# mLSTM probabilities times scores: the scores read from PSUM by VectorE instead of from a copy made by ScalarE

## What is computed

```
dmat = where(causal, b[t] - b[s] + i[s], -inf)
s    = einsum('bhtd,bhsd->bhts', q, k) * exp(dmat - mt[t])     # scores times probabilities
num  = einsum('bhts,bhsd->bhtd', s, v) + sc * einsum('bhtk,bhkv->bhtv', q, C)
den  = sum(s) + sc * einsum('bhtk,bhk->bht', q, n)
h    = num / max(|den|, exp(-mt))
```

## Time and profile before

| quantity | us |
|---|---|
| median of 3 runs | 1116.43 |
| lowest and highest of them | 1115.91 and 1117.73 |
| span of the profiled execution, first to last instruction | 1115.5 |
| busy TensorE / VectorE / ScalarE / GpSimd in it | 1048.6 / 317.7 / 196.8 / 97.2 |

### The profile page before, as it was taken

One profiled execution on the slowest core, in us unless ns is written; L12 is line 12 of the kernel. 1 busy time (PEld: TensorE's weight loads), 2 busy tenths in 40 slices (PEclk: granted clock), 3 DMA queues, 4 the chain that ended last, 5 costly groups with the idle time before them and its releaser, 6 DMA issues.

```text
span 1115.5 us, 13239 instructions
## 1 busy us (share of the span) xinstructions
PE 1048.6 (94%) x5164; PEld 440.2 (39%) x5164; DVE 317.7 (28%) x639; ACT 196.8 (18%) x412; POOL 97.2 (9%) x179
## 2 busy tenths in 40 slices
PE   8999999999999999899899999999899988998996
PEld 5667755433433343333233323342324332433332
DVE  6778454421222212121121212121212120202123
ACT  5433613610201020002010201010002000100002
POOL 7887300000000000000000000000000000000000
PEclk9999999999999999999999999999999999999999
DMA  7531689999999999999999999999999999999995
GB/s 235 173 114 33 197 328 379 384 423 429 433 430 428 432 430 432 432 431 432 432 430 431 432 431 432 431 431 432 432 429 432 431 431 432 431 431 432 424 427 211
DMA packets 62051, 429.45 MB, mean 385 GB/s; under 512 B 12022, under 2 KB 25054, under 8 KB 33342
## 3 DMA queue, kind: packets, MB, share of 16 engines
q1 hardware_dynamic: 60868, 428.16, 91.9%
q10 hardware_dynamic: 1146, 0.79, 0.3%
HBM read 424.68 MB, written 3.67 MB: 384 GB/s over the span
## 4 chain that ended last, share of the span: by engine, by line
PE 61%; DMA 35%; DVE 2%; ACT 1%; issue 1%; SPq 1%; ACTq 0%; DVEq 0%
DMA ring_a<-in_exp_w_dram 26%; PE psum L2374 16%; PE psum L2409 13%; DMA ring_b<-in_exp_w_dram 8%; PE psum L2395 7%; PE psum L1825 4%; PE psum L2308 4%; PE psum L2137 3%; PE psum L2331 3%; PE psum L1837 3%; PE psum L2418 1%; PE psum L2258 1%; PE psum L2264 1%; SPq L438 0%; PE psum L2424 0%
## 5 line engine op out<-in xcount | busy, mean ns | idle before, releaser
L2374 PE MATMUL psum<-ring_a,xg 128*64 128x512 f32 x1200 | 341.8, 600 | 14.8 <-DMA ring_a<-in_exp_w_dram 14.8
L2409 PE MATMUL psum<-ring_a,aT 128*64 128x512 f32 x768 | 217.7, 596 | 9.0 <-DMA ring_a<-in_exp_w_dram 8.8
L2374 PEld LDWEIGHTS psum<-ring_a,xg 128*64 128x64 f32 x1200 | 102.9, 137 | 170.4 <-issue 166.5
L2374 PE MATMUL psum<-ring_b,xg 128*64 128x512 f32 x368 | 152.3, 598 | 7.7 <-DMA ring_a<-in_exp_w_dram 7.7
L1640 DVE TENSOR_TENSOR x<-x,psum 128x512 f32<-128x512 f32 x64 | 44.0, 688 | 383.1 <-PE psum L2331 383.1
L2395 PE MATMUL psum<-ring_a,xg 128*64 128x512 f32 x336 | 105.3, 614 | 13.2 <-DMA ring_b<-in_exp_w_dram 13.2
L2409 PEld LDWEIGHTS psum<-ring_a,aT 128*64 128x64 f32 x768 | 68.3, 137 | 110.9 <-issue 105.6
L2409 PE MATMUL psum<-ring_b,aT 128*64 128x512 f32 x256 | 104.1, 595 | 3.6 <-ACT aT L1027 1.8
L1709 DVE TENSOR_SCALAR acts<-psum 128x512 f32<-128x512 f32 x32 | 22.0, 687 | 223.0 <-PE psum L2395 207.7
L2374 PEld LDWEIGHTS psum<-ring_b,xg 128*64 128x64 f32 x368 | 43.1, 136 | 75.4 <-issue 62.7
L1023 ACT ACTIVATE acts<-acts 128x512 f32<-128x512 f32 x32 | 20.1, 627 | 296.1 <-DVE acts L1709 296.1
(11 more groups left out here) (493 smaller groups left out, 943.1 us busy)
## 6 DMA issues: line engine op xcount, KB each, us to landing
ring_a<-in_exp_w_dram SPq DMA_DIRECT2D x144, 2048.0 KB, 26.3
ring_b<-in_exp_w_dram SPq DMA_DIRECT2D x46, 2048.0 KB, 24.8
ring_a<-in_w_in_dram SPq DMA_DIRECT2D x4, 2048.0 KB, 8.6
ring_a<-in_w_out_dram SPq DMA_DIRECT2D x2, 2048.0 KB, 9.5
ring_a<-in_w_in_dram SPq DMA_DIRECT2D x3, 1024.0 KB, 6.0
ring_a<-in_state_ml_c_dram SPq DMA_DIRECT2D x4, 512.0 KB, 6.4
out_dram<-ring_a SPq DMA_DIRECT2D x4, 512.0 KB, 6.5
ring_b<-in_exp_w_dram SPq DMA_DIRECT2D x2, 1024.0 KB, 28.7
```

What stands on the lines that cost most here:

```text
L2374: m = M(psum[64 * x:64 * x + 64, bk, :], xg[:, k, u, 64 * x:64 * x + 64], w[x][:, 512 * bk:512 * bk + 512], start=False, stop=(k == KD - 1))
L2409: m = M(psum[64 * x:64 * x + 64, 4 + nn, :], aT[:, 2 * j + s, 64 * x:64 * x + 64], w[x][:, 1024 * s + 512 * nn:1024 * s + 512 * nn + 512], ...
```

## The change

ScalarE's four copies of `st{h}` into `stS` go, and the buffer `stS` with them, so that two small buffers (`smpS`, `scS`) move to a lower address. VectorE's product reads the scores from the bank itself, waits for the exponential (`mb{h}` drained) and for the fill of `st{h}`, and is now what drains `st{h}`.

```diff
-        stS, smpS, scS = carve(ra, [128, H, 384]), carve(ra, [128, TS]), carve(ra, [128, H, TS])
+        smpS, scS = carve(ra, [128, TS]), carve(ra, [128, H, TS])
...
                 A(E[:, h, 256:384], bank(f"mb{h}")[:, 256:384], ACT.Exp, scale=-1.0, bias=rtok[:, 1, h:h + 1]).then_inc(
                     drained[FILLS[f"mb{h}"][0]], 1)
-                copy_out(f"st{h}", stS[:, h, :], bank(f"st{h}")[:, 0:384])
...
             def e_prob(h):
-                b, f = FILLS[f"st{h}"]
+                b, f = FILLS[f"mb{h}"]
                 dve.wait_ge(drained[b], f + 1)
-                says(TT(E[:, h, :], stS[:, h, :], E[:, h, :], ALU.mult), "e_ready", h + 1)
+                await_fill(dve, f"st{h}")
+                drains(TT(E[:, h, :], bank(f"st{h}")[:, 0:384], E[:, h, :], ALU.mult), f"st{h}")
+                dve.sem_inc(says_now("e_ready"), 1)
```

## The result

| | median us | lowest to highest | ratio to before, 95% interval |
|---|---|---|---|
| before, beside the first comparison | 1116.72 | 1115.91 to 1117.73 | |
| changed, first comparison | 1119.55 | 1119.31 to 1121.77 | 1.0031 [1.002, 1.0041] |
| changed, second | 1119.24 | 1117.56 to 1120.47 | 1.0017 [1.0008, 1.0025] |
| changed, third | 1119.28 | 1117.64 to 1121.55 | 1.0016 [1.0007, 1.0025] |

By the ratios the changed kernel is slower by 0.16 to 0.31%, 1.8 to 3.5 us; the median of the kernel before beside the second and the third comparison was 1116.81 us. Single executions of one kernel spread by more than this difference: 35 of the kernel before went from 1115.76 to 1119.53 us. The profile of the first comparison is of an execution of 1121.22 us, the second longest of its six.

The account below looks back on a forecast made before the run. TensorE was taken to bound the changed stretch and the weight stream the experts. Saved copies and VectorE time count 0; a new TensorE wait of 1.43 us added to 1116.43 gives 1117.9 us, range 1116.0 to 1120.6.

Parts of the forecast that it names:

- held product: Rival: GpSimd still holds VectorE's product at 1.78 us; TensorE waits at `st3` and `vb1`, 4.0 us, 1120.4 us; chance 0.13.
- What bounds the kernel, and that nothing is gained: TensorE alone carries the changed stretch, the weight stream the experts; removing four ScalarE copies, 2.0 us in all, is worth 0.
- The first expert step moves the end one for one: Whatever moves TensorE's first expert step at 199.86 us moves the end by as much, the weight stream behind being fixed.
- The product takes 0.56 us: VectorE's product reading PSUM takes 0.56 us at each head instead of 1.78, not held by GpSimd.
- VectorE's queue: Instructions ahead of `e_prob(2)`, three held by GpSimd, put that product at 109.27 to 109.83 us, after TensorE wants `st3`.
- The new wait: TensorE begins `st3` at 109.93 us instead of 108.50, waiting for VectorE's product to drain `st2`: 1.43 us.
- No second wait at `vb1`: `e_prob(3)` ends at 114.9 us, before TensorE wants the bank for `vb1` at 115.80.
- the missed hold: Rival: L1369 misses its slot; `s5_value(0)` is held by one GpSimd instruction more; wait 2.3 us, 1118.7 us; chance 0.18.
- a wait at zero: Rival: `s5_value(0)` is not held, `e_prob(2)` ends by 108.3 us before TensorE comes; 1116.4 us; chance 0.13.
- faster: Rival: VectorE's 1.2 us saved at each product reaches TensorE, 1 to 3 us, about 1114 us; chance 0.06.
- The step from span to time: The median of the runs was taken to stand 0.9 us above the profiled span.

Follow-up runs that it names:

- e2: Changed kernel with the three SBUF instructions of `s5_value(0)` moved behind `e_prob(3)` in VectorE's queue: 1116.81 us, ratio 0.9994 to the kernel before.
- e3: Kernel before, copies kept, with one added wait: TensorE waits for the end of `s5_scan(6)` before `st3`; 1120.16 us, ratio 1.0027.
- e5: Changed kernel with the change undone for head 2 alone (ScalarE copies `st2` again): 1119.36 us, ratio 1.0020 to the kernel before.
- e6: Changed kernel with the change undone for heads 2 and 3: 1117.30 us, ratio 0.9999 to the kernel before.
- e10: Repeat of the kernel before with TensorE's added wait for the end of `s5_scan(6)` before `st3`: 1120.24 us, ratio 1.0025.
- e1: Changed kernel with 14 small bf16 matmuls of TensorE in front of the wait for `st3`: 1119.74 us, ratio 1.0024 to the kernel before.
- e7: Changed kernel with 21 small bf16 matmuls of TensorE in front of the wait for `st3`: 1118.56 us, ratio 1.0015 to the kernel before.

## Why the prediction was right in its mechanism and short in its size

The measured time, 1119.55 us, lies inside the range 1116.0 to 1120.6 and outside the forecast's own range, 1117.2 to 1118.6. That it lies inside the wide range is partly luck: the upper part stood there for a held product, which did not come. The shift against before was forecast as +1.43 us; the ratios of the three comparisons give +3.5, +1.9 and +1.8 us. I gave 0.66 to no measurable difference and 0.28 to slower, and it is slower, with the last two comparisons just under my 0.2% and the first above it.

- *What bounds the kernel, and that nothing is gained:* right. Copies and VectorE's time went, and in e2, where all four copies are gone and no wait is left, no gain shows.
- *The first expert step moves the end one for one:* right. It came 3.72 us later in the first profile and the span grew by 3.9. With a wait in the kernel before (e3) it came 4.28 us later and the span grew by 4.6.
- *The product takes 0.56 us:* right, 0.56 at each head, from L1400 and L1402 of before. The Trainium skill, SBUF — State Buffer, section "SBUF: two separate sides", says that a VectorE instruction with two SBUF inputs and a GpSimd instruction that reads SBUF exclude each other. The traces agree: the form with a PSUM operand took 0.56 us beside L699, and in e5 the form with two SBUF operands began 0.04 us behind L699 and ended 0.41 us behind its end.
- *VectorE's queue:* right in its sum, with errors that cancelled. The gap before the product is 0.24 us, not 0.17. L1368 was not held as I had it, to 0.32 us behind L699's end: it began 0.04 us before that end and ran its 0.46 us, which brought it out at nearly the same time. L1369 and L1370 were each held by the GpSimd instruction I named. Product 2 began 0.70 us behind TensorE's wish for the bank, and I had 0.77.
- *The new wait:* 1.32 us against 1.43, at `st3` and only there. The semaphore took 0.06 us, not 0.1. No second wait at `vb1`, as worked out.
- *The rivals:* the missed hold did not come, the held product neither (e5, where one product has its old form, shows what one would have done: a wait at `vb1`), a wait at zero did not come, and faster did not.
- *What I left out:* I treated a wait as costing its own length. TensorE's idle can be followed by a fall of its clock to 1.2 GHz, and the matmuls behind it then take 5.3 us instead of 3.6. The hint was in the table I read: the 0.99 from 210 to 1105 us is an average over five falls to 0.50, the first right behind an idle of TensorE. I took it for a constant. With 1.7 us in one execution of three, as in the three profiles of the changed kernel, the forecast would have been 2.0 us above before instead of 1.4. This is the mis-sized term.
- *The step from span to time:* the profiled execution of before was not a typical one. In every later profile the time of the execution lies 1.7 to 1.9 us above its span (e6: 1117.28 for the same span of 1115.5), not 0.9. As the shift was added to the median, this moved nothing.

What stays open is when the clock falls. Idle time alone does not decide: 1.12 to 1.15 us was followed by a fall once in three, 1.56 us before `st3` once in two, 1.56 us before `vb1` never in two, the 1.31 us ahead of the first long row of matmuls in some profiles and not in others, and there was a fall at 79 us in a run of work that was almost the same in the kernel before. Nor is its frequency known. A count of 2 in 5 would put the changed kernel at about 2.0 us and does not fit the first comparison well, whose interval begins at 2.2 us. The ratios of e3 and e10, 3.0 and 2.8 us, exceed their wait of 1.6 by most of a fall, which would mean more falls than one in two; their intervals are too wide to say so.

## What to carry to other kernels

Before an operand is moved from a copy to its PSUM bank, ask who drains the bank now, and what stands ahead of that in its queue. Here an idle engine's copy of 0.49 us was the early release, and the busy engine's product, 1.2 us faster, was a late one. If the product is worth having, move what stands ahead of it (e2) rather than the copy back in one place (e5), which only moved the wait. And where a table shows a clock of 0.99 over a long stretch, ask for shorter stretches: it can be an average over falls to half, and a new wait can put one where it costs.

## What the runs showed of the hardware that I had not expected

- The granted clock went to 0.50 for about 3.4 us and came back, in some executions of a kernel and not in others, with the wait ahead of it the same to 0.01 us. Each such fall in a row of matmuls lengthened it by 1.6 to 1.7 us: `vb0` 5.30 against 3.62 us, the 32 matmuls at 13 us 9.69 against 8.00, the 16 at 79 us 5.79 against 4.15 in the kernel before, the 32 of the last expert 8.8 against 7.1.
- The kernel before has such falls too, five between 210 and 1105 us, and every other profile has some in that stretch.
- With TensorE's wait filled with small bf16 matmuls (e1, e7) the clock was 1.00 there in both profiles. With falls in 2 of 5 without them, this is not shown to be their doing.
- VectorE's L1368, with two SBUF operands, started 0.04 us before the end of GpSimd's L699 in the changed kernel and ran at its full speed (0.46 us). The product with two SBUF operands started 0.04 us behind the start of L699 and took 1.78 us. The recorded times of GpSimd's instructions are rough, so the 0.04 us say no more than "at about the same time".
